# A hybrid diffusion layer with a 32-expert MoE: router logits taken from the raw residual, and the gathered rows turned for half of the experts

## What is computed

```python
def rmsnorm(x, g):
    y = xf * lax.rsqrt(jnp.mean(xf * xf, axis=-1, keepdims=True) + EPS)
    return (y * g.astype(F32)).astype(x.dtype)

def layer(x, cond, h0, on_grid, p):
    ...
    mix, h_last = token_mixer(h, h0, on_grid, p)
    x = x + g1 * mix
    h = rmsnorm(x, p['g_norm2']) * (1 + sc2) + sh2
    x = x + g2 * hier_moe(h, p)

def hier_moe(h, p):
    lg = (t @ p['w_router_group'] + p['b_router_group']).astype(F32)
    grp = jnp.argmax(lg, axis=-1)
    le = (t @ p['w_router_expert'] + p['b_router_expert']).astype(F32)
    le_g = jnp.take_along_axis(le.reshape(-1, N_GROUPS, EXPERTS_PER_GROUP), grp[:, None, None], axis=1)[:, 0]
    top_p, top_i = lax.top_k(jax.nn.softmax(le_g, axis=-1), TOP_K)
    ...
    for e in range(N_EXPERTS):
        z = jax.nn.silu(t @ p['w1'][e]) * (t @ p['w3'][e])
        y = y + gates[:, e:e + 1] * (z @ p['w2'][e])
```

## Time and profile before

| quantity | value |
|---|---|
| median of 3 runs | 990.8 us (990.57 to 993.1) |
| the profiled execution, its own time | 991.51 us |
| its span, first to last instruction | 989.2 us |
| TensorE busy | 872.0 us, 88% |
| VectorE busy | 603.7 us, 61% |
| ScalarE busy | 279.2 us, 28% |
| GpSimd busy | 248.8 us, 25% |
| bytes moved by DMA | 285.71 MB, mean 289 GB/s |

### The profile page before, as it was taken

The page is one execution under the profiler, slowest core; times in us unless marked ns, Lnnn a source line. Parts: engine busy times, 40 slices in busy tenths (PEclk is TensorE's granted clock), DMA queues, the critical chain, the costliest instruction groups (busy, mean ns, idle before and its releaser), DMA issues.

```text
span 989.2 us, 12334 instructions
## 1 busy us (share of the span) xinstructions
PE 872.0 (88%) x4438; PEld 548.4 (55%) x4438; DVE 603.7 (61%) x977; ACT 279.2 (28%) x469; POOL 248.8 (25%) x207
## 2 busy tenths in 40 slices
PE   3898898998999999996899999999888888888892
PEld 1688796987999999644533333333333333333330
DVE  2589696859202542157347777676766666666676
ACT  4474535573233432022112111211111111111112
POOL 0047362636255555000211111110111101010000
PEclk9899999999999999997799999999999999999996
DMA  9953182745564356718299999999999999999931
GB/s 344 358 215 119 52 262 87 254 161 194 177 234 170 118 201 219 311 68 307 100 392 409 410 418 411 418 427 402 396 413 407 412 400 417 408 411 423 415 145 66
DMA packets 59639, 285.71 MB, mean 289 GB/s; under 512 B 6692, under 2 KB 11076, under 8 KB 47300
## 3 DMA queue, kind: packets, MB, share of 16 engines
q1 hardware_dynamic: 55764, 278.11, 72.2%
q0 software_dynamic: 2560, 3.15, 1.1%
q10 hardware_dynamic: 1264, 3.76, 1.0%
HBM read 287.06 MB, written 3.19 MB: 293 GB/s over the span
## 4 chain that ended last, share of the span: by engine, by line
PE 52%; DMA 22%; DVE 16%; ACT 5%; issue 3%; DVEq 0%; POOL 0%; ACTq 0%
PE bank L935 13%; DMA slot<-in_w 10%; DMA ring<-in_w 10%; PE bank L948 7%; PE bank L783 6%; PE bank L784 6%; PE bank L785 6%; PE bank L835 3%; DVE xcy L1485 3%; DVE xcy L1823 2%; DMA ring<-in_w_in 2%; DVE cp L1568 1%; PE bank L936 1%; DVE lru L1539 1%; PE bank L921 1%
## 5 line engine op out<-in xcount | busy, mean ns | idle before, releaser
L458 POOL TENSOR_TENSOR subs<-ring,subs 128x1024 fp32r<-128x1024 f32 x69 | 177.2, 2575 | 218.0 <-ACT subs L1061 218.0
L783 PE MATMUL bank<-h_hl,subs 128*128 128x384 f32 x488 | 167.5, 343 | 12.0 <-ACT lru L1140 4.6
L785 PE MATMUL bank<-h_hl,subs 128*128 128x384 f32 x488 | 165.5, 339 | 0.0
L784 PE MATMUL bank<-h_hl,subs 128*128 128x384 f32 x488 | 165.5, 339 | 0.0
L1798 DVE TENSOR_TENSOR lru<-bank,cp 128x512 f32<-128x512 f32 x192 | 125.3, 678 | 1.0
L1807 DVE TENSOR_TENSOR hg<-hg,lru 128x512 f32<-128x512 f32 x192 | 125.2, 677 | 0.0
L935 PE MATMUL bank<-ring,x_T 128*64 128x512 f32 x256 | 113.0, 594 | 11.4 <-DMA ring<-in_w 5.4
L936 PE MATMUL bank<-ring,x_T 128*64 128x512 f32 x256 | 113.3, 595 | 0.0
L633 POOL COPY idx<-lists 64x1 uint32 (+1 forms) x32 | 5.7, 177 | 413.8 <-PE bank L899 334.7
L783 PEld LDWEIGHTS bank<-h_hl,subs 128*128 128x128 f32 x488 | 92.8, 190 | 19.3 <-issue 9.6
L1061 ACT ACTIVATE subs<-ring 128x1024 fp32r<-128x1024 f32 x72 | 76.1, 1060 | 68.3 <-PE bank L785 65.5
(11 more groups left out here) (226 smaller groups left out, 1381.8 us busy)
## 6 DMA issues: line engine op xcount, KB each, us to landing
ring<-in_w SPq DMA_DIRECT2D x48, 2048.0 KB, 29.3
slot<-in_w SPq DMA_DIRECT2D x36, 2048.0 KB, 27.2
ring<-in_w_in SPq DMA_DIRECT2D x14, 2048.0 KB, 8.4
ring<-in_w_ada SPq DMA_DIRECT2D x12, 2048.0 KB, 8.8
gate_w<-in_w SPq DMA_DIRECT2D x12, 2048.0 KB, 27.6
ring<-in_w_rnn_out SPq DMA_DIRECT2D x2, 2048.0 KB, 8.5
ring<-in_w_conv_out SPq DMA_DIRECT2D x2, 2048.0 KB
ring<-in_w_o SPq DMA_DIRECT2D x2, 2048.0 KB, 8.4
```

The source lines that it names most:

```text
L458: eng.tensor_tensor(pair[:, 1], src, pair[:, 0].bitcast(F32), ALU.subtract).then_inc(done, 1)
L783: eng.matmul(ps[:, 0:T], pair[:, 1, k, :], x[:, 0, k, :], start=(k == 0), stop=False)
L784: eng.matmul(ps[:, 0:T], pair[:, 0, k, :], x[:, 1, k, :], start=False, stop=False)
L785: mm = eng.matmul(ps[:, 0:T], pair[:, 0, k, :], x[:, 0, k, :], start=False, stop=(k == KD - 1))
```

## The change

Four things are changed, and the program's order around the end of the mixer with them.

1. The logits are formed from the residual x1 itself. Since h2 is x1 times 1/rms times a gain per column plus a shift per column, the gain is multiplied into the router's weights (`wr_gain`, one copy for each of the two conditions, two VectorE operations on 128x288), the shift's part of the logits is a constant row (`rc`, 16 float32 products of 36 columns on TensorE, between the two halves of `yb`), and 1/rms is multiplied in when the logits leave PSUM. So x1, not h2, is turned (`x1T`), in contiguous blocks; h2 is kept in its natural column order, and the experts' transposes now read the gathered rows in steps of 32 bytes.
2. `choose` sets the logits of other groups to -3e38 and takes one maximum over all 32, in place of multiplying out the chosen group's 8.
3. One-hots of the slot and of the token are prepared on GpSimd (`places`), ahead of the comparison with the rank on VectorE.
4. For experts 16 to 31 the slot is 63 minus the rank, so their lists are filled from slot 63 downward.

The diff, cut to its core (the list `WO_ON` and the calls in their new order are shown as they are built below):

```diff
-    stream += [("modT",)]
+    stream += [("modT",), ("rc",)]
...
+        wr_gain = sb("wr_gain", [P, 2, KD, NG + NE])
...
-        token_col = [sb(f"token_col{s}", [P, 1]) for s in range(4)]
+        token_col = sb("token_col", [P, 4])
...
-                    rows_of(wr[:, :, 0:NG], w_router_group[0].rearrange("(p k) n -> p k n", p=P), router_in)
+                    rows_of(wr[:, :, 0:NG], w_router_group[0].rearrange("(k p) n -> p k n", p=P), router_in)
...
-            eng.wait_ge(h2_ready, 2 * TT)
+            eng.wait_ge(h2_ready, TT)
             load(2, 2, 1)
             load_mod(3, G2)
...
+            def places(t):
+                r = rt[:, t, :]
+                eng.wait_ge(both_ready, t + 1)
+                then(eng.tensor_scalar(r[:, 52:54], r[:, 46:48], float(NE // 2), 2.0, ALU.is_lt, ALU.mult))
+                eng.tensor_scalar(r[:, 50:52], r[:, 46:48], float(NE // 2), float(CAP - 1), ALU.is_ge, ALU.mult)
+                then(eng.tensor_scalar(r[:, 52:54], r[:, 52:54], -1.0, None, ALU.add))
+                for k in range(2):
+                    eng.tensor_scalar(rank_oh[:, t, k, :, :], iota[:, 0:CAP].unsqueeze(1).to_broadcast([P, 2, CAP]),
+                                      r[:, 52 + k:53 + k], r[:, 50 + k:51 + k], ALU.mult, ALU.add)
+                for k in range(2):
+                    last = eng.tensor_scalar(tok_oh[:, t, k, :], pick[:, t, k, :], tok[:, k, t:t + 1], None, ALU.mult)
+                last.then_inc(places_ready, 1)
...
+            def router_constants():
+                ps = open_tile(("rc",))
...
+                for cnd in range(2):
+                    for k in range(KD):
+                        mm = eng.matmul(ps[:, 64 * cnd:64 * cnd + NG + NE], mod2[:, cnd, 1, k:k + 1].to_broadcast([P, P]),
+                                        wr[:, k, :], start=(k == 0), stop=(k == KD - 1))
...
             project("yb", 0, hs_hl, ready=hs_split)
             transpose_mod()
+            router_constants()
             project("yb", 1, hs_hl)
...
-            def transpose_h2(t, half):
-                eng.wait_ge(h2_ready, 2 * t + half + 1)
+            def transpose_x1(t, half):
+                eng.wait_ge(x1_ready, 2 * t + half + 1)
...
-                    mm = eng.matmul(ps[:, 0:NG + NE], h2T[:, k, :], wr[:, k, :],
+                    if k % 4 == 0:
+                        wait_read(eng, ("x1T", t, k // 4))
+                    mm = eng.matmul(ps[:, 0:NG + NE], x1T[:, k, :], wr_gain[:, 0 if t == 0 else 1, k, :],
...
-                rows = xg[:, s, :].rearrange("t (k p) -> t k p", k=KD)
+                rows = xg[:, s, :].rearrange("t (p k) -> t k p", k=KD)
...
+            for cnd in range(2):
+                eng.tensor_tensor(wr_gain[:, cnd, :, :], wr[:, :, :],
+                                  mod2[:, cnd, 2, :].unsqueeze(2).to_broadcast([P, KD, NG + NE]), ALU.mult)
...
+                then(eng.scalar_tensor_tensor(out=h2[:, t % 2, :], in0=x_rows[:, t, :],
+                                              scalar=stat[:, 1, 0, t:t + 1], in1=A2[:, cnd, :],
+                                              op0=ALU.mult, op1=ALU.mult))
+                eng.tensor_tensor(h2[:, t % 2, :], h2[:, t % 2, :], B2[:, cnd, :], ALU.add).then_inc(h2_ready, 1)
...
+                eng.scalar_tensor_tensor(out=le[:, t, :], in0=ps[:, NG:NG + NE], scalar=stat[:, 1, 0, t:t + 1],
+                                         in1=rc[:, cnd, NG:], op0=ALU.mult, op1=ALU.add).then_inc(free, 1)
...
-                then(eng.tensor_scalar(r[:, 40:40 + NG], iota[:, 0:NG], r[:, 36:37], None, ALU.is_equal))
-                then(eng.tensor_scalar(r[:, 16:24], le[:, t, 0:EG], r[:, 40:41], None, ALU.mult))
-                for g in range(1, NG):
-                    then(eng.scalar_tensor_tensor(out=r[:, 16:24], in0=le[:, t, g * EG:(g + 1) * EG],
...
+                then(eng.tensor_scalar(r[:, 40:40 + NG], iota[:, 0:NG], r[:, 36:37], -3.0e38, ALU.not_equal, ALU.mult))
+                then(eng.tensor_tensor(le[:, t, :].rearrange("p (g e) -> p g e", g=NG),
...
+                then(eng.max(r[:, 24:32], le[:, t, :]))
...
+                eng.wait_ge(places_ready, t + 1)
                 for k in range(2):
-                    last = eng.tensor_scalar(rank_oh[:, t, k, :, :], iota[:, 0:CAP].unsqueeze(1).to_broadcast([P, 2, CAP]),
+                    last = eng.tensor_scalar(rank_oh[:, t, k, :, :], rank_oh[:, t, k, :, :], rank[:, t, k:k + 1],
```

More of the change, by code:

```diff
@@ L1296, in top_exps @@
                 eng.activation(rt[:, t, 34:35], rt[:, t, 35:36], ACT.Exp).then_inc(texp_ready, 1)
-            norm_rows(0)
-            route_copies(0)
-            norm_rows(1)
-            route_copies(1)
-            norm_rows(2)
-            route_copies(2)
+            square(0)
+            root(0)
+            x1_copy(0, 0)
+            x1_copy(0, 1)
+            square(1)
+            root(1)
+            store(0)
+            x1_copy(1, 0)
+            x1_copy(1, 1)
+            x1_copy(2, 0)
+            square(2)
+            x1_copy(2, 1)
+            root(2)
+            store(1)
+            store(2)
             for t in range(TT):
@@ L1630, in _, with router_constants @@
             ada_columns(11)
+            eng.wait_ge(router_in, 32)
+            eng.wait_ge(gain_ready, 2)
+            for cnd in range(2):
+                eng.tensor_tensor(wr_gain[:, cnd, :, :], wr[:, :, :],
+                                  mod2[:, cnd, 2, :].unsqueeze(2).to_broadcast([P, KD, NG + NE]), ALU.mult)\
+                    .then_inc(wr_ready, 1)
+            def router_constants():
+                ps, free = tile(("rc",))
+                eng.wait_ge(bias_in, 32)
+                for cnd in range(2):
+                    last = eng.tensor_tensor(rc[:, cnd, :], ps[:, 64 * cnd:64 * cnd + NG + NE], br[:, :], ALU.add)
+                last.then_inc(free, 1)
             for k in range(KD):
+                if k == CT:
+                    router_constants()
                 ps, free = tile(("yb", k))
@@ L1645, in _, with residual @@
                 eng.tensor_tensor(SA[:, k, :], SA[:, k, :], SB[:, k, :], ALU.add).then_inc(merged_ready, 1)
-            def residual(t):
+            def residual(t, half):
                 cnd = 0 if t == 0 else 1
-                for half in range(2):
-                    cols = slice(half * CW, (half + 1) * CW)
-                    ps, free = tile(("wo", t, half))
-                    eng.tensor_tensor(wo_tmp, ps[:, :], G1[:, cnd, cols], ALU.mult).then_inc(free, 1)
-                    eng.wait_ge(free, N_OF[("wo", t, half)] // BANKS + 1)
-                    ins = eng.tensor_tensor(x_rows[:, t, cols], x_rows[:, t, cols], wo_tmp, ALU.add)
-                    if half == 0:
-                        then(ins)
-                ins.then_inc(x1_ready, 1)
+                cols = slice(half * CW, (half + 1) * CW)
+                ps, free = tile(("wo", t, half))
+                if half or t:
+                    eng.wait_ge(x1_ready, 2 * t + half)
+                eng.tensor_tensor(wo_tmp, ps[:, :], G1[:, cnd, cols], ALU.mult).then_inc(free, 1)
+                eng.wait_ge(free, N_OF[("wo", t, half)] // BANKS + 1)
+                eng.tensor_tensor(x_rows[:, t, cols], x_rows[:, t, cols], wo_tmp, ALU.add).then_inc(x1_ready, 1)
@@ L1680, in norm2 @@
-                then(last)
-                for half in range(2):
-                    eng.tensor_tensor(h2_half[half], h2_half[half], blocks(B2[:, cnd, :], half), ALU.add)\
-                        .then_inc(h2_ready, 1)
+                then(eng.scalar_tensor_tensor(out=h2[:, t % 2, :], in0=x_rows[:, t, :],
+                                              scalar=stat[:, 1, 0, t:t + 1], in1=A2[:, cnd, :],
+                                              op0=ALU.mult, op1=ALU.mult))
+                eng.tensor_tensor(h2[:, t % 2, :], h2[:, t % 2, :], B2[:, cnd, :], ALU.add).then_inc(h2_ready, 1)
@@ L1715, in choose @@
                     .then_inc(both_ready, 1)
-                for k in range(2):
-                    last = eng.tensor_scalar(tok_oh[:, t, k, :], pick[:, t, k, :], tok[:, k, t:t + 1], None,
-                                             ALU.mult)
+                eng.tensor_scalar(r[:, 32:33], r[:, 8:9], -1.0, None, ALU.mult)
+                eng.tensor_tensor(r[:, 35:36], r[:, 25:26], r[:, 24:25], ALU.subtract)\
+                    .then_inc(tops_ready, 1)
             def weights(t):
@@ L1748, in _ @@
             eng.wait_ge(consts, 6)
-            residual(0)
+            residual(0, 0)
+            residual(0, 1)
+            mean(0)
+            over_root(0)
             norm2(0)
-            residual(1)
-            norm2(1)
-            choose(0)
-            residual(2)
+            residual(1, 0)
+            choose(0)
+            residual(1, 1)
+            mean(1)
+            over_root(1)
+            residual(2, 0)
+            norm2(1)
+            place(0)
+            choose(1)
+            residual(2, 1)
+            place(1)
+            mean(2)
```

(6 more changed lines are left out.)

121 lines of the change are left out of this document (67 added, 54 removed).

## The result

The changed kernel takes **996.09 us** (median of 12 runs, 994.99 to 998.98) against 992.41 us of the kernel before, measured beside it (12 runs, 990.57 to 993.95): ratio **1.0041, 95% interval 1.0032 to 1.005**. It is slower by 0.4%, where a gain of 4.6 us was forecast, and outside the range. Three executions that took half as long again or longer (two of experiment 17, one of the kernel before beside it) are left out of its median and ratio. Its profiled execution took 998.98 us (span 997.2), the longest of the twelve.

The account below looks back on a forecast made before the run. The weight stream was taken as the bound: when expert 0's product starts it and how long it lasts. Start +2.9 and turned rows -7.5 gave -4.6 us on the profiled 991.51, rounded with its offset from the median 990.8 to 986.2; range 981 to 992.

Parts of the forecast that it names:

- What bounds the kernel: Experts' stage: the gapless weight stream paces it, so expert 0's product end and the stream's length count.
- Constant row, +3.6: 16 more float32 products on a full TensorE delay all that follows up to expert 0 by 3.6 us.
- h2, store, GpSimd's wait: Tile 2's h2 ready at 468.1; its store lands 9.2 us later beside a load, so GpSimd begins gathering at 477.4.
- The list, 472.2: List of gathered rows ready at 472.2, before 476.6; 0.4 us added to VectorE's norm for meeting GpSimd's operations.
- Clock, +2.2: TensorE idles some 5 us before expert 0, then runs 3.6 us at half clock: 2.2 us lost, between 0 and 3.6.
- Start of the stream, +2.9: Expert 0 starts 0.7 us later and loses 2.2 to the clock; its product ends at 492.2 instead of 489.3.
- Strided transposes, about 0: Experts' transposes in 32-byte steps: 0.77 us becomes 1.3 at factor 1.7, covered by idle time and waits for weights.
- Turned rows, -7.5: Turning experts 16 to 31 nearly closes the staircase of DMA engines at stream's end: 7.5 of its 8.9 us won.
- The prediction's own sign for the turn: At the stream's end, DMA share falls from full to nothing within some 4 us instead of 15.
- Rival 3: The turn does not do what it says (staircase has another cause, or engines picked otherwise than by slot): 993.7, chance 0.08.

Follow-up runs that it names:

- experiment 17: The kernel with the three edits, the slot of every expert being rank + 16: 994.53 us, ratio 1.0023 to the kernel before.
- Experiment 6: Changed kernel; SyncE's load that reuses the second norm's memory waits until expert 0's rows have been gathered: 990.56 us, ratio 0.9977 to the kernel before.
- experiment 1: Changed kernel with no expert turned (slot = rank for all 32), every instruction kept: 995.51 us, ratio 1.0027 to the kernel before.
- experiment 4: Changed kernel with the constant row's 16 products spread over the first tile of yb's second half: 995.78 us, ratio 1.0033 to the kernel before.
- experiment 2: Changed kernel with the experts' transposes reading gathered rows in contiguous blocks again (right column order left out): 994.89 us, ratio 1.0028 to the kernel before.
- the three edits: Changed kernel with load behind expert 0's gather, constant row's products spread, tile 2's norm ahead of its choice: 989.86 us with the turn, 989.14 without.
- experiment 3: Changed kernel; SyncE's load that reuses the second norm's memory waits until the third store of h2 has landed: 994.09 us, ratio 1.0017 to the kernel before.

## Why the prediction was wrong

By its own steps:

- **What bounds the kernel: right.** The stream from expert 0's product to the end. Experiment 6 only issues one load and the transfer behind it later; the product then ends at 488.1 instead of 494.4 (experiment 1), and the time falls by 0.64%, 6.4 us. The waits for weights add up to 21.7 us, not 18.9, since 2.8 us on `gate_w` were left out; nothing in the sum rests on it.
- **Constant row, +3.6: right.** 54.4 less 50.8 is 3.6 (experiment 4).
- **h2, store, GpSimd's wait: right.** Forecast for the third store 468.1 and for GpSimd 477.4; in experiment 1 469.37 and 479.51, in an execution that was already 1.5 us late at the modulation rows. The store landed in 10 us beside the load.
- **The list, 472.2: wrong, without consequence.** The 0.4 us was put on the wrong engine. VectorE's norm was not stretched (1.28 and 1.22 us); GpSimd's first two operations beside it were (1.34 and 1.15 us for 0.25), and VectorE's one-hots then waited 1.71 us for GpSimd. The list was read at 475.2; the store came later still.
- **Clock, +2.2: right.** In experiment 1 the granted clock was 0.50 from 485.6 to 488.2, and expert 0's product took 8.8 us (485.6 to 494.4) instead of 7.1.
- **Start of the stream, +2.9: right.** The changed kernel without the turn is slower by 0.27%, 2.7 us, in the medians (5.1 us between the two profiled executions, of which 1.5 is there at 357 us).
- **Strided transposes, about 0: right**, and for the reason given: 0.35 us more at a factor of 1.45, not 1.7, and the idle time behind it takes it up (experiment 2). The Trainium skill (SBUF — State Buffer, the note on "cachelines") says that reads which share no 16-byte line lose rate. For TensorE the trace agrees in kind (1.12 us for 0.77); the price is lower than in VectorE's rows.
- **Turned rows, -7.5: this is the step that failed.** Measured: -1.7 us on the kernel before (0.6 longer, less 2.3 us of its later start), +1.4 in the changed kernel, +0.9 with the three edits, each with an uncertainty of over 1 us: nothing, within 2 us. The prediction took the same rows in other slots to cost the same, and turned all of the unevenness into time. In other slots the whole stream runs slower (some 2.4 us for sixteen experts), and of 8.9 us evening out gave back about 1.5. With 0 to +1.4 in place of -7.5 the sum is a change of +2.9 to +4.3; measured are 996.09 - 992.41 = +3.7. A further 1.6 of the 9.9 us between forecast and time lie in the base: 990.8 was the median of 3 runs, that of 12 is 992.41.

The prediction's own sign for the turn, a much shorter fall, came true (6 to 9 us for 15, where 4 was forecast), and the gain did not: the sign did not test the term. Rival 3 (the turn does not do what it says, 993.7) was nearest and had 0.08, but only its number was near: its reason, another cause of the staircase, is refuted by the shorter fall. It was argued against by "nothing else is dealt unevenly", which says where the staircase comes from and not what removing it costs.

## What to carry to other kernels

A staircase at the end of a stream is no reserve of its full length: level it and ask for the mean rate as well as for the length of the fall, since the mean may come to the last instead of the last to the mean. A small store on which a chain waits should not be issued together with a megabyte load; but look at what the load meets next: here the first step, behind the store, gave 0.24%, and the second, behind the gather too, another 0.40%. Where one execution is read, compare the clock with a second one before a drop is explained.

## What had not been expected of the hardware

- A gather's slots are not alike: at equal rows, equal busy share (1.00 to 1.01) and all experts alike, 402 and 406 GB/s with slots shifted by 8, 411 and 411 unshifted, while the gathers' own share stayed at 2.2%.
- Float32 products with 2 columns of weights: 16 passes in 0.7 us of busy time, where 32 with 128 columns took 3.7. A load of weights took 88 ns for 2 columns and 191 for 128. The 128 were one column repeated; the logits, with 128 different ones, took as long (48 passes in 5.9). So with 36 moving columns in all of them, the width of the weights made the difference.
- A load of 2 MB issued beside it stretched a store to 10 us (2.6 with the load behind it, experiment 3), and a gather's way from index to transposes from 4.0 to 7.7.
